# Filler products between the gated levels, a retention output in five parts, and another order on VectorE and GpSimd

## The chip, the cores and the metric

The kernel runs on one core of one Trainium2 chip. The metric is the device time of one execution in microseconds (us). A core has five engines with instruction queues of their own: TensorE (PE in the profile; PEld is its weight load), VectorE (DVE), ScalarE (ACT), GpSimd (POOL) and SyncE (SP), which here only issues transfers. Each runs its instructions in program order, and they wait for one another through semaphores. TensorE's clock has two levels in the profile, 2.4 GHz (granted clock 1.00) and 1.2 GHz (0.50).

## The reference

The reference is two blocks of two layers on 512 tokens of width 1024, all in float32. The change lies in the layers of the first block, and there between the attention and the output projection. Such a layer computes

```python
proj = h @ w_in                                   # aq ak av ag | rq rk rv rg | gq gk gv gg ga
a_out = sliding_window_attention(aq, ak, av, sinks) * silu(ag)
r = retention(rq, rk, rv)                         # 4 heads, chunks of 128 tokens
r_out = rms_norm(r) * silu(rg)
log_a = log_sigmoid(ga @ gla_gate_w + gla_gate_b) / 16
g = gated_linear_attention(gq, gk, gv, log_a)     # 4 heads of 32, chunks of 64 tokens
g_out = rms_norm(g, gla_norm_gain) * silu(gg)
y = concatenate([a_out, r_out, g_out]) @ w_out
x = x + gate * rms_norm(y, post_gain)
```

Retention scans over chunks: `intra` is the masked product of the chunk's queries and keys times its values, `inter` is the decayed queries times a 64x64 state per head that is carried from chunk to chunk. Gated linear attention does the same with a decay of its own for every token and channel: `sc[i, j] = sum_d q[i, d] exp(b[i, d] - b[j, d]) k[j, d]` with b the running sum of log_a. The second block (two layers, each with attention and a feed-forward part) is not touched.

## The kernel before, in words

The program is a list of phases written by hand, and each phase writes the instructions of each engine in a fixed order; there is no scheduler. In a layer of the first block the phases are: norm and transposes, the projection `w_in`, transposes of heads, the attention, the class `Memories` (retention and gated attention), the projection `w_out` and the residual. `Memories` is the subject. It runs once in each of two layers (246 to 295 us and 556 to 606 us of the profile).

The gated scores are computed in six levels, `LEVELS = (32, 16, 8, 4, 2, 1)`, from the far pairs of tokens to neighbours. For level l GpSimd forms distances (`distance`, L2939 and L2940), ScalarE their exponentials (`factor`, L2891), VectorE scales the queries (`scale_queries`, L2787) and GpSimd the keys (L2960). TensorE multiplies them (`level_scores`, L2613: 16 products of 32 rows by 64 columns), and the result is put into the score tile: the first two levels by ScalarE (`copy_level`, L2768), the other four by VectorE (`place`, L2779). The scores of a level go into the same PSUM banks 0 to 3 as those of the level before, so a level waits until that one has been placed. Diagonal scores come first (`own_scores` L2601, `place_own` L2757).

Between the levels TensorE does other work: after level 0 it transposes the decayed keys (L2706, which wait for `g_kd`, L2854, on VectorE), after level 1 come the state updates (`gated_updates`, L2624), after level 2 the whole retention output (`retention_out`: L2586 with the carried states, then L2593 with the chunk's own scores, 16 products that show as 32 records), after level 4 the transposes of the attention output (`mix_turn`, L2653). After level 5 `gated_out` (L2637, L2641) waits for the last `place`. A float32 product is two records in the profile.

Around it: `retained` (L2565) and `keep_retained` (L2726) are the chunk scores of retention, R0 and R1; `retained_updates` (L2575) and `retained_states` (L2731, L2734) its states; `gated_states` (L2744, L2746) those of the gated part; `retained_gates` (L2797) and `retained_means` (L2802) work on the retention output. The groups of `GROUP_NAMES` are results in the PSUM banks 2 and 4 to 7; `open` waits until the group that last used the bank has been taken out of it (kept). `keep_clock(pe, n)` (L254) issues n products of 128 rows by 256 columns whose result nobody reads, by default into bank 7. `weights_low` (L321) splits a weight unit on GpSimd.

## Time and profile before

| | |
|---|---|
| Time, median of three runs | 2465.29 us (2464.46 to 2468.06) |
| The profiled execution | 2465.29 us, span 2463.4 us |
| Busy | PE 2294.8 us (93%), PEld 1972.0 (80%), DVE 1426.3 (58%), ACT 962.4 (39%), POOL 944.0 (38%) |
| Mean granted clock of TensorE | 0.964 |
| First layer's `Memories` | log transposes at 245.21 us, level 0 at 254.87, `gated_out` at 287.19, output projection at 295.18 |
| Second layer's `Memories` | level 0 at 565.36 us, `gated_out` at 597.75 |

A row of the timeline has the start in the span and the duration in us, the engine, the line of the kernel, the operation, what it writes and reads, and in brackets the idle time ahead of it with what ended it. The two layers run the stage alike, 310.5 us apart.

### The profile page before, as it was taken

The page shows a single profiled execution, that of the slowest core. Times are in us where ns is not written, and L with a number is a line of the kernel's source. Part 1 is how long each engine was busy: PE and PEld are TensorE (multiplying, and loading weights), DVE is VectorE, ACT ScalarE, POOL GpSimd, SP SyncE. Part 2 cuts the span into 40 slices and gives each one's busy share as a digit, 9 for nine tenths or more (in the row PEclk, how much of TensorE's full clock was granted, in tenths as well). Part 3 has the DMA queues.
Part 4 walks back from the last instruction along what each step waited for, and adds up shares of the span by engine and source line. Part 5 has one row for each costly group of instructions (what it writes and reads, how often), then busy time and mean ns, then how long its engine had stood idle before and what let it go on. Part 6 is the DMA issues. An engine that isn't in the chain of part 4 may idle for free.

```text
span 2463.4 us, 36101 instructions
## 1 busy us (share of the span) xinstructions
PE 2294.8 (93%) x14294; PEld 1972.0 (80%) x14294; DVE 1426.3 (58%) x2032; ACT 962.4 (39%) x1818; POOL 944.0 (38%) x740
## 2 busy tenths in 40 slices
PE   4998899988899889899999999999899999899998
PEld 4787777877778556679989989898787767789987
DVE  6865536655777654475515234134677765757756
ACT  2335242352234756624221212113425873534433
POOL 3443464434353423416433424334652433321022
PEclk9999699996899999999999999999999999999999
DMA  9650035201433000031423323233441004233332
GB/s 310 192 164 18 19 107 185 86 18 44 145 105 116 2 1 1 10 120 32 135 74 95 103 76 96 86 94 98 147 137 34 1 1 137 78 110 105 95 103 77
DMA packets 163999, 219.11 MB, mean 89 GB/s; under 512 B 19381, under 2 KB 102741, under 8 KB 163705
## 3 DMA queue, kind: packets, MB, share of 16 engines
q1 hardware_dynamic: 163832, 216.82, 28.0%
q8 instruction: 114, 1.87, 0.3%
q14 instruction: 53, 0.43, 0.1%
HBM read 214.69 MB, written 2.10 MB: 88 GB/s over the span
## 4 chain that ended last, share of the span: by engine, by line
PE 56%; DVE 5%; ACT 3%; POOL 2%; issue 2%; DMA 0%; ACTq 0%; DVEq 0%; POOLq 0%; SPq 0%
PE ps L336 14%; PE ps L338 13%; PE ps L337 13%; PE ps L1198 5%; PE ps L1226 4%; PE ps L1248 2%; PE ps L1506 1%; DVE mod_acc_aux L435 1%; PE ps L1245 1%; POOL h_transposed L653 1%; PE ps L461 1%; PE ps L665 0%; ACT att_probs_two L1291 0%; ACT att_probs_lat L1291 0%; PE ps L1501 0%
## 5 line engine op out<-in xcount | busy, mean ns | idle before, releaser
L321 POOL TENSOR_TENSOR w_lo<-w_raw,w_hi 128x1024 fp32r<-128x1024 f32 (+3 forms) x205 | 479.9, 2342 | 1040.1 <-ACT w_hi L315 1040.0
L315 ACT ACTIVATE w_hi<-w_raw 128x1024 fp32r<-128x1024 f32 (+3 forms) x232 | 234.2, 1012 | 836.8 <-PE ps L338 762.6
L336 PE MATMUL ps<-w_hi,h_transposed 128*128 128x512 f32 (+3 forms) x1136 | 422.0, 372 | 25.7 <-POOL w_lo L321 11.7
L337 PE MATMUL ps<-w_lo,h_transposed 128*128 128x512 f32 (+3 forms) x1136 | 413.7, 364 | 0.0
L338 PE MATMUL ps<-w_hi,h_transposed 128*128 128x512 f32 (+3 forms) x1136 | 413.4, 364 | 0.0
L336 PE MATMUL ps<-h_transposed,w_hi 128*128 128x384 f32 (+2 forms) x1048 | 337.0, 322 | 8.0 <-POOL h_transposed L653 3.3
L338 PE MATMUL ps<-h_transposed,w_lo 128*128 128x384 f32 (+2 forms) x1048 | 335.9, 321 | 0.0
L337 PE MATMUL ps<-h_transposed,w_hi 128*128 128x384 f32 (+2 forms) x1048 | 335.9, 320 | 0.0
L336 PEld LDWEIGHTS ps<-w_hi,h_transposed 128*128 128x128 f32 x1136 | 219.3, 193 | 64.4 <-POOL w_lo L321 15.6
L337 PEld LDWEIGHTS ps<-w_lo,h_transposed 128*128 128x128 f32 x1136 | 219.4, 193 | 32.2 <-issue 2.2
L338 PEld LDWEIGHTS ps<-w_hi,h_transposed 128*128 128x128 f32 x1136 | 218.9, 193 | 32.0
L336 PEld LDWEIGHTS ps<-h_transposed,w_hi 128*128 128x128 f32 x1048 | 197.9, 189 | 11.4 <-issue 3.8
L337 PEld LDWEIGHTS ps<-h_transposed,w_hi 128*128 128x128 f32 x1048 | 197.9, 189 | 1.4
L338 PEld LDWEIGHTS ps<-h_transposed,w_lo 128*128 128x128 f32 x1048 | 197.9, 189 | 1.3
L1330 DVE TENSOR_REDUCE attention_stats<-ps 128x1 f32<-128x768 f32 (+5 forms) x192 | 143.8, 773 | 51.5 <-PE ps L1198 43.9
L435 DVE SCALAR_TENSOR_TENSOR mod_acc_aux<-mod_units_one,c_act,mod_acc_aux 128x512 f32<-128x512 f32 x128 | 133.2, 1058 | 42.3 <-DMA mod_units_one<-in_w_mod_dram 31.5
L336 PE MATMUL ps<-w_hi,ffn_hidden 128*128 128x512 f32 x384 | 154.8, 403 | 0.6 <-DVE ffn_hidden L1948 0.6
L338 PE MATMUL ps<-w_hi,ffn_hidden 128*128 128x512 f32 x384 | 153.6, 400 | 0.0
L337 PE MATMUL ps<-w_lo,ffn_hidden 128*128 128x512 f32 x384 | 153.5, 400 | 0.0
L1705 DVE TENSOR_TENSOR ffn_full<-ps,ffn_silu 128x768 f32<-128x768 f32 x22 | 20.0, 953 | 184.2 <-PE ps L338 184.2
L435 DVE SCALAR_TENSOR_TENSOR mod_acc_gates<-w_raw,c_act,mod_acc_gates 128x512 f32<-128x512 f32 x98 | 114.9, 1207 | 12.8 <-DMA w_raw<-in_ada_w_dram 11.2
L336 PEld LDWEIGHTS ps<-w_hi,ffn_hidden 128*128 128x128 f32 x384 | 73.4, 191 | 18.5 <-POOL w_lo_third L321 1.0
(399 smaller groups left out, 4240.2 us busy)
## 6 DMA issues: line engine op xcount, KB each, us to landing
w_raw<-in_ffn_w_in_dram SPq DMA_DIRECT2D x88, 512.0 KB, 3.6
w_raw<-in_ada_w_dram SPq DMA_DIRECT2D x48, 512.0 KB, 4.0
w_raw<-in_ffn_w_out_dram SPq DMA_DIRECT2D x44, 512.0 KB, 3.8
mod_units_one<-in_w_mod_dram SPq DMA_DIRECT2D x80, 256.0 KB, 4.3
w_raw<-in_w_in_dram SPq DMA_DIRECT2D x40, 512.0 KB, 3.8
w_raw<-in_w_out_dram SPq DMA_DIRECT2D x16, 512.0 KB, 4.5
mod_units_one<-in_ada_w_dram SPq DMA_DIRECT2D x32, 256.0 KB, 4.1
mod_unit_even<-in_ada_w_dram SPq DMA_DIRECT2D x16, 512.0 KB, 3.8
```

The costliest lines, as they stand in the source:

```text
L315: act.activation(split_room(i)[0][:, 0:k * n], src[:, 0:k * n], ACT.Copy).then_inc(w_hi_ready.sem, 1)
L321: eng.tensor_tensor(low, src[:, 0:k * n], high.bitcast(F32), ALU.subtract).then_inc(w_lo_ready.sem, 1)
L336: pe.matmul(acc, left[0], right[0], start=start, stop=False, skip_group_check=shared)
L337: pe.matmul(acc, left[0], right[1], start=False, stop=False, skip_group_check=shared)
L338: return pe.matmul(acc, left[1], right[0], start=False, stop=stop, skip_group_check=shared)
L435: ins = dve.scalar_tensor_tensor(out=like(self.acc[:, r]), in0=view[:, j], scalar=c_act[:, cond, 2 * q + j, c:c + 1], in1=like(first if q ...
L461: ins = pe.matmul(ps[:, 6 + m % 2, 4 * i + j:4 * i + j + 1], self.acc[:, i, j * P:(j + 1) * P], ones[:, 0:1], start=True, stop=True)
L653: pool.tensor_tensor(HT[:, 1, kt, tiles[0] * P:tiles[0] * P + n], self.whole(g, kt, tiles), hi.bitcast(F32), ALU.subtract).then_inc(ht_low ...
L1198: done.append(pe.matmul(sc[:, c:c + m], x["q"][i], x["keys"][i][k][0], start=True, stop=not masks))
L1226: ins = pe.transpose(ps[:, self.turn_bank(r), i * P:(i + 1) * P], self.probs[s % len(self.probs)][:, c:c + P], ident)
L1248: ins = pe.matmul(ps[64 * i:64 * i + 64, self.SUM_BANK, 0:P], v[i], probs_t[:, (i * nb + b) * P:(i * nb + b + 1) * P], start=(b == 0), sto ...
L1330: ins = dve.tensor_reduce(dst, src, AX, ALU.max, negate=True)
```

## The change

- **Fillers.** `keep_clock` is called nine times: 3 products before level 0, 1 before and 2 after the transposes of the keys, 2 after the gated updates, 2 after level 2, 1 before level 4, 2 before and 1 after level 5. That is 14 products in each layer.
- **Retention output in five parts.** `retention_carried` after level 2, then four parts of `retention_out(par, two)`: one after level 2, two after level 3, one after level 4. The transposes of the attention output move from before level 5 to behind it.
- **Banks.** The groups have a table of banks (`BANKS`), and `AFTER` names for each the group that must have been taken out first. RU (the retention updates) moves to bank 7 and ahead of SUMS on TensorE. The second bank of the retention output now is the one that held the gated updates, so it opens after `gated_states`; before it opened after the kept keys.
- **VectorE.** `retained_states`, `place_own` and `scale_queries(0)` come before `g_far` (L2849); `keep_retained(R1)` and `scale_queries(1)` before `g_kd`; `place(2)` before `gated_states`; `place(4)` before `retained_gates`.
- **GpSimd.** The second of two `weights_low` moves from the start of the stage behind the gains of level 3. **ScalarE:** `factor(1)` moves before the exponential of `g_far`.

```diff
+            BANKS = [2, 4, 5, 6, 7, 4, 5, 6, 4, 5, 6, 4, 5, 0, 1, 2, 3]
+            AFTER = {SUMS: LOG, R1: R0, R1 + 1: R0 + 1, KD: SUMS, GU: R1, GU + 1: R1 + 1, RO: KD, RO + 1: GU}
+            MIX_BANKS = [6, 4, 5, 7, 0, 1, 2, 3]
+            MIX_AFTER = [GU + 1, RO, RO + 1, RU, OUT, OUT + 1, OUT + 2, OUT + 3]
...
             def open(self, pe, g):
-                if g >= 5:
-                    self.wait_kept(pe, g - 4)
+                if g in self.AFTER:
+                    self.wait_kept(pe, self.AFTER[g])
                 return self.bank(g)
...
-            def retention_out(self, pe):
+            def retention_carried(self, pe):
                 banks = [self.open(pe, self.RO + par) for par in range(2)]
                 self.wait_kept(pe, self.RU)
...
-                self.wait_kept(pe, self.R1 + 1)
-                for par in range(2):
-                    for t in range(XT):
-                        for pair in range(2):
-                            c, v0 = pair * 256 + t * 64, RV + 64 * (2 * pair + par)
-                            ins = pe.matmul(banks[par][:, c:c + 64], ret_a[:, t, par, tok(pair)], P1[:, t, v0:v0 + 64], start=False,
-                                            stop=(t == XT - 1 and pair == 1), skip_group_check=True)
+            def retention_out(self, pe, par, two):
+                self.wait_kept(pe, (self.R1 if two else self.R0) + 1)
+                for t in (2 * two, 2 * two + 1):
+                    for pair in range(2):
+                        c, v0 = pair * 256 + t * 64, RV + 64 * (2 * pair + par)
+                        ins = pe.matmul(self.bank(self.RO + par)[:, c:c + 64], ret_a[:, t, par, tok(pair)], P1[:, t, v0:v0 + 64], start=False,
+                                        stop=(two == 1 and t == XT - 1 and pair == 1), skip_group_check=True)
+                if two:
                     ins.then_inc(mem_made.sem, 1)
...
                 self.retained(pe, self.R1, 1)
+                self.wait_kept(pe, self.RU)
+                keep_clock(pe, 3)
                 self.wait(pe, mem_cleared, 1)
                 for l in range(len(LEVELS)):
                     self.level_scores(pe, l)
                     if l == 0:
                         kd_tok = self.open(pe, self.KD)
+                        keep_clock(pe, 1)
                         self.wait(pe, k_out_ready, 1)
...
+                        keep_clock(pe, 2)
                     if l == 1:
                         self.gated_updates(pe)
+                        keep_clock(pe, 2)
                     if l == 2:
-                        self.retention_out(pe)
+                        keep_clock(pe, 2)
+                        self.retention_carried(pe)
+                        self.retention_out(pe, 0, 0)
+                    if l == 3:
+                        self.retention_out(pe, 1, 0)
+                        self.retention_out(pe, 0, 1)
+                        keep_clock(pe, 1)
                     if l == 4:
+                        self.retention_out(pe, 1, 1)
+                        keep_clock(pe, 2)
+                    if l == 5:
+                        keep_clock(pe, 1)
                         for kt in range(4):
...
                 self.scale_queries(dve, 3)
+                self.place(dve, 2)
                 self.gated_states(dve)
-                self.place(dve, 2)
```

TensorE, first layer, from level 2 (the first rows) to level 3, before. L2586 is the carried part of the retention output, L2593 the chunks' own part.

```order
L2613 MATMUL ps<-proj_one,gla_k_level 128x64 [waits gla_placed] x3
L2613 MATMUL ps<-proj_one,gla_k_level 128x64 x12
L2586 MATMUL ps<-ret_states,ret_qdecay_t 128x64 [waits memory_kept_dve,memory_kept_act]
L2586 MATMUL ps<-ret_states,ret_qdecay_t 128x64 x11
L2593 MATMUL ps<-proj_one,ret_scores_t 128x64 [waits memory_kept_dve]
L2593 MATMUL ps<-proj_one,ret_scores_t 128x64 x15
L2613 MATMUL ps<-proj_one,gla_k_level 128x64 [waits gla_placed,gla_k_level,gla_q_level]
```

And now (L2616 are the level's products, L2587 and L2595 the two kinds of retention output, L254 the fillers):

```order
L2616 MATMUL ps<-proj_one,gla_k_level 128x64 [waits gla_placed] x3
L2616 MATMUL ps<-proj_one,gla_k_level 128x64 x12
L254 MATMUL ps<-static_constants 128x256 x2
L2587 MATMUL ps<-ret_states,ret_qdecay_t 128x64 [waits memory_kept_dve,memory_kept_act]
L2587 MATMUL ps<-ret_states,ret_qdecay_t 128x64 x11
L2595 MATMUL ps<-proj_one,ret_scores_t 128x64 [waits memory_kept_dve]
L2595 MATMUL ps<-proj_one,ret_scores_t 128x64 x3
L2616 MATMUL ps<-proj_one,gla_k_level 128x64 [waits gla_placed,gla_k_level,gla_q_level]
```

Two fillers stand between level 2 and the carried part, and only a quarter of the own part is left ahead of level 3.

VectorE, first layer, from the placing of the diagonal scores to `g_kd`, before (L2849 is `g_far`, L2757 `place_own`, L2854 `g_kd`, L2731 and L2734 the retention states, L2726 `keep_retained`):

```order
L2849 TENSOR_TENSOR gla_distance_to_end<-gla_log_decay_sums 128x512 [waits memory_kept_act]
L2757 TENSOR_TENSOR proj_one<-ps,constants_one 128x512 [waits gla_scored] x4
L2787 TENSOR_TENSOR proj_one<-gla_q_t,gla_factor 128x256 [waits gla_factor]
L2854 TENSOR_TENSOR gla_distance_to_end<-gla_k_t,gla_decay_out 128x512 [waits gla_decays_ready]
L2731 COPY ret_states<-ps 128x128 [waits memory_made]
```

And now, behind the retention states (L2770 is `place_own`, L2865 `g_far`, L2739 `keep_retained`, L2870 `g_kd`):

```order
L2770 TENSOR_TENSOR proj_one<-ps,constants_one 128x512 [waits gla_scored] x4
L2800 TENSOR_TENSOR proj_one<-gla_q_t,gla_factor 128x256 [waits gla_factor]
L2865 TENSOR_TENSOR gla_distance_to_end<-gla_log_decay_sums 128x512 [waits memory_kept_act]
L2739 TENSOR_TENSOR ret_scores_t<-ps,constants_one 128x2x256 [waits memory_made] x2
L2800 TENSOR_TENSOR proj_one<-gla_q_t,gla_factor 128x256 [waits gla_factor]
L2870 TENSOR_TENSOR gla_distance_to_end<-gla_k_t,gla_decay_out 128x512 [waits gla_decays_ready]
```

The scaling for level 0 no longer has `g_far` ahead of it, and `g_kd` has two keeps and the scaling for level 1 ahead of it.

VectorE, first layer, from the scaling of the queries of levels 2 and 3 to the placing of level 2, before (L2744 and L2746 are `gated_states`, L2779 is `place(2)`):

```order
L2787 TENSOR_TENSOR proj_one<-gla_q_t,gla_factor 128x256 [waits gla_scored,gla_factor] x2
L2744 COPY gla_states<-ps 128x64 [waits gla_decays_ready,memory_made]
L2746 SCALAR_TENSOR_TENSOR gla_states<-gla_states,gla_chunk_decay,ps 128x64 [waits dve_step] x6
L2779 COPY_PREDICATED proj_one<-constants_one,ps 128x32x8 [waits gla_placed,gla_scored] x4
L2787 TENSOR_TENSOR proj_one<-gla_q_t,gla_factor 128x256 [waits gla_scored,gla_factor]
```

And now (L2800, L2792, L2757 and L2759 in the same roles):

```order
L2800 TENSOR_TENSOR proj_one<-gla_q_t,gla_factor 128x256 [waits gla_scored,gla_factor] x2
L2792 COPY_PREDICATED proj_one<-constants_one,ps 128x32x8 [waits gla_placed,gla_scored] x4
L2757 COPY gla_states<-ps 128x64 [waits gla_decays_ready,memory_made]
L2759 SCALAR_TENSOR_TENSOR gla_states<-gla_states,gla_chunk_decay,ps 128x64 [waits dve_step] x6
L2800 TENSOR_TENSOR proj_one<-gla_q_t,gla_factor 128x256 [waits gla_scored,gla_factor]
```

The states, for which the carried part on TensorE now waits, stand behind the placing of level 2, and that waits for level 2.

## Rows read from the trace of the kernel before

**Rows 1.** The page: TensorE's granted clock in 40 slices, in tenths
```profile
PEclk9999699996899999999999999999999999999999
```

**Rows 2.** Stretches of both layers: start:end, busy us per engine, PEclk, DMA share, GB/s
```profile
243.00:256.00 13.00, 8.18 (x142) 7.08 (x140) 8.67 (x12) 5.69 (x10) 9.65 (x9) 1.00 0.01 1
257.00:267.00 10.00, 7.70 (x144) 7.25 (x144) 7.23 (x19) 4.88 (x10) 9.53 (x13) 0.50 0.01 2
267.00:276.00 9.00, 9.00 (x68) 8.76 (x66) 0.20 (x1) 1.19 (x2) 0.00 (x0) 0.50 0.01 2
...
284.00:287.00 3.00, 0.58 (x24) 0.45 (x16) 2.39 (x5) 0.00 (x0) 2.02 (x1) 1.00 0.53 199
288.00:297.00 9.00, 9.00 (x59) 8.53 (x49) 3.72 (x9) 1.53 (x4) 0.00 (x0) 0.50 0.01 2
...
568.00:594.00 26.00, 23.60 (x264) 22.32 (x264) 13.56 (x32) 7.57 (x15) 10.28 (x15) 0.50 0.26 78
```

**Rows 3.** Timeline, first layer: start us, us, instruction; in brackets the idle time before
```profile
254.87 1.12 PE L2613 MATMUL ps<-proj_one,gla_k_level 32*128 32x64 f32 x32 [2.98 <-DVE proj_one L2787]
...
258.70 1.98 PE L2613 MATMUL ps<-proj_one,gla_k_level 32*128 32x64 f32 x32 [1.97 <-DVE proj_one L2787]
...
262.55 1.99 PE L2613 MATMUL ps<-proj_one,gla_k_level 32*128 32x64 f32 x32 [0.60 <-ACT proj_one L2768]
...
264.46 2.83 PE L2586 MATMUL ps<-ret_states,ret_qdecay_t 64*128 64x64 f32 x24
...
267.21 7.09 PE L2593 MATMUL ps<-proj_one,ret_scores_t 128*128 128x64 f32 x32
...
276.81 2.87 PE L2613 MATMUL ps<-proj_one,gla_k_level 32*128 32x64 f32 x32 [0.59 <-DVE proj_one L2779]
...
279.61 3.67 PE L2653 MATMUL ps<-static_constants,proj_one 128*128 128x128 f32 x16
```

**Rows 4.** Timeline, first layer: the two kinds of product of gated_out
```profile
287.19 1.21 PE L2637 MATMUL ps<-gla_states,gla_gate_ln 32*64 32x64 f32 x56 [2.61 <-DVE proj_one L2779]
...
288.33 7.09 PE L2641 MATMUL ps<-proj_one 128*128 128x64 f32 x32
```

**Rows 5.** Timeline, first layer: VectorE around the levels
```profile
249.51 2.06 DVE L2849 TENSOR_TENSOR gla_distance_to_end<-gla_log_decay_sums 128x512 f32<-128x512 f32 x1 [1.19 <-ACT gla_log_decay_sums L2885]
...
251.49 2.47 DVE L2757 TENSOR_TENSOR proj_one<-ps,constants_one 128x512 f32<-128x512 f32 x4
...
253.88 0.88 DVE L2787 TENSOR_TENSOR proj_one<-gla_q_t,gla_factor 128x256 f32<-128x256 f32 x1
...
254.69 1.21 DVE L2854 TENSOR_TENSOR gla_distance_to_end<-gla_k_t,gla_decay_out 128x512 f32<-128x512 f32 x1
...
256.13 0.98 DVE L2734 SCALAR_TENSOR_TENSOR ret_states<-ret_states,constants_one,ps 128x64 f32<-128x64 f32 x4
...
257.03 1.28 DVE L2726 TENSOR_TENSOR ret_scores_t<-ps,constants_one 128x512 f32<-128x512 f32 x2
...
263.68 1.86 DVE L2746 SCALAR_TENSOR_TENSOR gla_states<-gla_states,gla_chunk_decay,ps 128x64 f32<-128x64 f32 x6
...
265.46 1.42 DVE L2779 COPY_PREDICATED proj_one<-constants_one,ps 128x256 f32<-128x256 uint32 x4
...
279.30 2.46 DVE L2779 COPY_PREDICATED proj_one<-constants_one,ps 128x256 f32<-128x256 uint32 x4
...
284.61 2.43 DVE L2779 COPY_PREDICATED proj_one<-constants_one,ps 128x256 f32<-128x256 uint32 x4 [1.60 <-PE ps L2613]
```

**Rows 6.** Timeline, TensorE: fillers (L254) and 64-column products at either clock
```profile
241.61 1.69 PE L254 MATMUL ps<-static_constants 128*128 128x256 f32 x4
...
243.13 1.00 PE L1239 MATMUL ps<-proj_one,att_probs_t_one 128*128 128x64 f32 x8
...
341.71 3.61 PE L254 MATMUL ps<-static_constants 128*128 128x256 f32 x16
```

**Rows 7.** Timeline, second layer: TensorE's wait after the output projection's first half
```profile
642.61 3.57 PE L461 MATMUL ps<-static_constants,mod_acc_aux 128*128 128x1 f32 x16 [6.46 <-ACT y_square_junk L1032]
```

More of the change, by code:

```diff
@@ L2528, in __init__ @@
                 self.bank_signal = ht_low
-                self.bank_done = {4 + kt: self.g0 + kt + 1 for kt in range(4)}
-                self.bank_done.update({kt: self.g0 + 5 + kt for kt in range(4)})
+                self.bank_done = {self.MIX_BANKS[kt]: self.g0 + kt + 1 for kt in range(KT)}
                 self.prelude_sp, self.prelude_dve = prelude_one(1) if l == 0 else prelude_even()
@@ L2690, in tensor @@
                 self.retained(pe, self.R0, 0)
+                self.retained_updates(pe)
                 sums = self.open(pe, self.SUMS)
@@ L2846, in vector @@
                 self.keep_retained(dve, self.R0, 0)
+                self.retained_states(dve)
+                self.place_own(dve)
+                self.scale_queries(dve, 0)
                 self.wait_kept(dve, self.SUMS)
@@ L2866, in vector @@
                 self.scale_queries(dve, 5)
+                self.place(dve, 4)
                 self.retained_gates(dve)
-                self.place(dve, 4)
                 self.retained_means(dve)
@@ L2943, in gpsimd @@
                 n = len(LEVELS)
-                for _ in range(2):
-                    weights_low(pool, 2, HALF)
+                weights_low(pool, 2, HALF)
                 self.wait(pool, mem_cleared, 1)
@@ L2965, in gpsimd @@
                             ins.then_inc(gains_ready.sem, 1)
+                            weights_low(pool, 2, HALF)
                 for i, c in enumerate((slice(0, 16), slice(16, 24), slice(24, 32))):
```

27 lines of the change are left out of this document (8 added, 19 removed).

## The prediction

> **What bounds the kernel now.** I read the page's clock row first, then stretches cut where the clock changes, then the timeline of the stage that is changed, first TensorE, then VectorE. The clock row shows a 6 at the fifth and the tenth slice and an 8 behind the tenth: those are the two layers' retention and gated stages [rows 1]. Cut finer, TensorE has 1.00 up to 256 us, 0.50 from 257 on through the levels and the retention output, 1.00 again for the short stretch 284 to 287, and 0.50 for the whole of `gated_out`; the second layer shows the same in 568 to 594 [rows 2]. In 267 to 276 TensorE is busy 9.00 of 9.00 us, nearly all of it the own part of the retention output, while VectorE works 0.20 us and GpSimd nothing [rows 2, 3]. So this stage has two faces: up to level 2 TensorE waits for the others (2.98 us ahead of level 0, 1.97 ahead of level 1, 0.60 ahead of level 2) [rows 3], from there to level 4 it is TensorE at half clock that everybody waits for, and at the end VectorE sets the pace: from the start of place(4) at 279.30 to the end of place(5) at 287.04, 7.74 us with 1.60 idle in it [rows 5], then `gated_out` at 287.19 [rows 4].
>
> A gain here reaches the end. Behind the stage TensorE is the engine that does not stop; the only wait of size is in the second layer, 6.46 us [rows 7], and it hangs on a chain of VectorE that begins after the stage's last transposes, so it moves with the stage.
>
> **Prices at the two clocks.** Four filler records, that is two products, took 1.69 us at half clock (0.85 a product); sixteen took 3.61 at full (0.45 a product). Eight records of 64 columns took 1.00 us at full [rows 6]; 32 of the same form took 7.09 at half, 1.77 for eight [rows 3]. A level's 32 records took 1.12 at full and 1.98 at half [rows 3]. The full clock is thus worth a factor of 1.8.
>
> **The change, step by step, first layer.**
>
> *Before level 0.* RU ahead of SUMS and its states on VectorE cost nothing: they lie in VectorE's 1.19 us of idle ahead of `g_far` [rows 5] (states 0.28 + 0.98); without that cover they would cost 1.3 us. place_own can start about 249.9 instead of 251.49 and takes 2.47, the scaling for level 0 took 0.88, so level 0 starts at about 253.3 instead of 254.87 [rows 3, 5]. The three fillers (3 x 0.45 = 1.4 us at full) lie in TensorE's idle time there. The second weights_low now runs where GpSimd has time; its unit is used two units of the projection later, no cost.
>
> *`g_kd` comes later.* After 253.3 VectorE has `g_far`, the R1 keep 1.28, a scaling about 0.4, `g_kd` 1.21. `g_far` took 2.06 beside the GpSimd split that is now gone; the same shape, `g_kd`, took 1.21 beside GpSimd's short operations [rows 5], and this is the nearer case: 1.2, bounds 0.7 (what two operations of the R1 keep take each, 0.64) and 2.1. Sum: 253.3 + 1.2 + 1.3 + 0.4 + 1.2 = 257.4. The key transposes wait for it, with level 1 queued behind them. With the one filler ahead, TensorE stands idle for most of the 3 us before 257.4, as it does now before 254.87 and 258.70; I expect the clock to fall at the same place, around 256.5. The transposes (about 0.9 at half) and two fillers (1.7) then put level 1 at 260.0, against 258.70.
>
> *The clock comes back early.* Transposes and fillers are the wide products beside which it returned before (242 us: fillers; 283 us: transposes of 128 columns) [rows 3, 6], and 2.6 us of them are one behind the other. At full clock the way from the start of level 1 to that of level 2 shrinks from 3.85 us (262.55 - 258.70) by 0.9 to 3.0, so level 2 begins near 263 and ends near 264.
>
> *A new wait.* The carried part writes to the bank of the gated updates and so waits for gated_states, which VectorE now does after place(2), which waits for level 2: 1.42 + 0.21 + 1.86 = 3.5 us after level 2 [rows 5], minus 0.9 for the two fillers: 2.6 us idle. The carried part begins at 267.4 instead of 264.46 [rows 3]; queued behind it are all products to the end. I expect the clock to fall a second time around here.
>
> *To the end of level 4.* From the carried part to place(4) it was 279.30 - 264.46 = 14.84. Off: one quarter of the own part 1.77, the wait 0.59 ahead of level 4 and the 0.9 by which level 4 (2.87 against 1.99) was slowed by the placing. On: a filler 0.85. That is 12.4, so place(4) starts at 279.8.
>
> *The tail.* place(4) to the end of place(5): the retention gates move into the 1.60 us idle, so 7.4 to 7.7, and `gated_out` starts at 287.4, 0.2 later than now. TensorE has in that time a quarter 1.77, two fillers 1.7, level 5, a filler and the sixteen transposes 3.67: this ends in time only if the clock is back by about 283.6, right after the two fillers. The transposes now stand directly ahead of `gated_out` instead of level 5 and an idle 2.61 us, so the clock is still full in it: 1.2 + 7.09 x 1.00 / 1.81 = 5.1 instead of 8.2, 3.1 less. The projection's first 1.9 us at half clock go, 0.9 less [rows 2, 4].
>
> *Sum.* +0.2 - 3.1 - 0.9 = -3.8 us a layer. In the second layer the same if the clock changes at the same steps. It need not: the same steps at half clock lose most of it (if it comes back only during the transposes, these end at 290, and 2.7 of the 3.8 go). I count two thirds there, 2.5. Together -6.3, and 2465.3 (the profiled execution: span 2463.4 and 1.9 around it, equal to the median) gives 2459.0. All edits with unknown size are in the range: `g_far` at 2.1 puts +0.9 on each layer, at 0.7 takes 0.5 off.
>
> **Rivals.**
>
> B. *The clock holds, or returns early and stays.* Level 1 at 258.8, level 2 at 261.8, carried part at 266.5; 12.4 at full clock is about 6.7, place(4) at 273.2, `gated_out` at 280.7: -6.5 and the 4.0 of the tail, 10.5 a layer: 2444.3. For it: fourteen fillers. Against it: the two idle stretches before 257.4 and before 267.4 stay, and 3.0 us of idle time is what preceded the fall at 256. The Trainium skill ("TensorE: Matmul & The Clock Gate", Part 1) says that the gate follows how busy TensorE has been and that activity releases it; by that alone this rival would be the likely one, since from the carried part on TensorE hardly stops. The trace disagrees: 9.00 busy of 9.00 us went by at 0.50 with the 64-column products [rows 2].
>
> C. *Slower: the fillers are paid at half clock.* If the clock does not come back after the key transposes, level 1 is at 260.0, level 2 at 263.9, the carried part at 269.4, place(4) at 281.8 and its end 289.3. TensorE after level 4 has 1.77 + 1.7 + 1.99 + 0.85 + 3.67 = 10.0 and reaches `gated_out` at 292.1, 4.9 later. If `gated_out` then runs at half too, both layers cost 9.8: 2475. If it runs at full, 0.9 a layer: 2467. It decides from the point where the clock is still 0.50 when `gated_out` begins. For it: the fillers are 8.5 us at half clock in the part that was never idle. Against it: the transposes brought the clock back before.
>
> D. *One gain, one loss.* The clock is back in one layer in time, in the other during the transposes or later: -3.8 and -1.1 to +4: 2460 to 2466, no change that can be told.
>
> **How the numbers follow.** What can be told from no change is 0.2%, 4.9 us. Forecast 0.40 (own range 2454 to 2463), B 0.12, C 0.18 (0.06 of it at the 2467 end), D 0.30. Faster: 0.40 x 0.9 + 0.12 + 0.30 x 0.2 = 0.54. Slower: 0.12 of C and 0.03 for mishaps of D: 0.15. Same: 0.31. The range runs from near B's end to just over C's cheap end, 2446 to 2469, and leaves out about half of B and 0.1 of C.
>
> **What would show it.** Right: level 0 near 253.3, key transposes near 257.4, an idle time of about 2.6 us ahead of the carried part ended by the state update on VectorE, place(4) near 279.8, `gated_out` near 287.4 and 5 us long at clock 1.00. Wrong: the clock at 1.00 through levels 3 and 4 (B), or 0.50 in `gated_out` (C); no idle time ahead of the carried part would void the step of the new wait.

## The result, and the profile after

The changed kernel took 2469.77 us (median of 20 runs, 2463.80 to 2474.43), the kernel before in the same job 2464.38 us (20 runs, 2460.53 to 2468.08): ratio 1.0020, 95% interval 1.0013 to 1.0028. The forecast was 2459.0, faster. It went the other way by 0.20%, and the time lies just above the range. All times and ratios here are of executions in the chip's faster state; one of e13's twelve, 3050.75 us at a granted clock of 0.70, is left out of its ratio. The profiled execution has a span of 2469.2 us against 2463.4.

The page's clock row after (tenths of full speed, 40 slices) still has its low places at the fifth, tenth and eleventh slice, as in [rows 1]:

```profile
PEclk9999799997899999999999999999999999999999
```

Stretches of the changed kernel, in the columns of [rows 2]:

```profile
239.00:249.00 10.00, 8.93 (x55) 7.85 (x56) 2.33 (x5) 6.27 (x8) 4.09 (x4) 0.50 0.00 0
249.00:259.00 10.00, 6.99 (x112) 5.62 (x108) 9.20 (x18) 4.92 (x9) 7.67 (x11) 1.00 0.01 2
260.00:262.00 2.00, 2.00 (x9) 1.17 (x12) 0.90 (x2) 0.60 (x1) 2.00 (x3) 0.50 0.00 0
263.00:269.00 6.00, 4.31 (x108) 3.21 (x102) 3.05 (x10) 2.65 (x6) 3.59 (x4) 1.00 0.01 3
270.00:293.00 23.00, 23.00 (x176) 20.34 (x176) 10.78 (x22) 3.62 (x6) 5.64 (x5) 0.50 0.17 49
294.00:297.00 3.00, 3.00 (x28) 3.00 (x28) 0.85 (x2) 0.93 (x3) 0.00 (x0) 1.00 0.00 0
584.00:607.00 23.00, 22.98 (x176) 20.58 (x176) 10.79 (x22) 3.51 (x6) 5.87 (x5) 0.50 0.24 71
```

In this execution the clock came back early, as forecast (1.00 in 263 to 269), but not for long. From 270, where the carried part is at work, it is 0.50 for 23 us, in which TensorE is busy 23.00 of 23.00 us; the second layer shows the same. It is full again in `gated_out`, which was at 0.50 before.

TensorE's timeline in the first layer, answering to [rows 3, 4] (L2616 are the levels, L2711 the key transposes, L254 the fillers, L2587 the carried and L2595 the own part, L2657 the mix transposes, L2640 and L2644 `gated_out`, L336 the output projection):

```profile
252.68 1.56 PE L254 MATMUL ps<-static_constants 128*128 128x256 f32 x6
254.78 1.12 PE L2616 MATMUL ps<-proj_one,gla_k_level 32*128 32x64 f32 x32 [0.54 <-DVE proj_one L2800]
255.83 0.70 PE L254 MATMUL ps<-static_constants 128*128 128x256 f32 x2
259.07 1.08 PE L2711 MATMUL ps<-static_constants,gla_distance_to_end 128*128 128x128 f32 x4 [2.54 <-DVE gla_distance_to_end L2870]
259.94 1.92 PE L254 MATMUL ps<-static_constants 128*128 128x256 f32 x4
261.79 1.47 PE L2616 MATMUL ps<-proj_one,gla_k_level 32*128 32x64 f32 x32
...
265.12 1.12 PE L2616 MATMUL ps<-proj_one,gla_k_level 32*128 32x64 f32 x32
266.17 1.13 PE L254 MATMUL ps<-static_constants 128*128 128x256 f32 x4
269.78 2.83 PE L2587 MATMUL ps<-ret_states,ret_qdecay_t 64*128 64x64 f32 x24 [2.48 <-issue]
...
279.82 1.17 PE L254 MATMUL ps<-static_constants 128*128 128x256 f32 x2
...
284.60 2.02 PE L254 MATMUL ps<-static_constants 128*128 128x256 f32 x4
...
288.46 1.22 PE L254 MATMUL ps<-static_constants 128*128 128x256 f32 x2
289.48 3.62 PE L2657 MATMUL ps<-static_constants,proj_one 128*128 128x128 f32 x16
293.03 0.95 PE L2640 MATMUL ps<-gla_states,gla_gate_ln 32*64 32x64 f32 x56
293.91 3.79 PE L2644 MATMUL ps<-proj_one 128*128 128x64 f32 x32
297.50 0.48 PE L336 MATMUL ps<-w_hi,h_transposed 128*128 128x512 f32 x1
...
300.81 0.50 PE L336 MATMUL ps<-w_hi,h_transposed 128*128 128x512 f32 x1 [1.67 <-DVE h_transposed L2666]
```

Two idle stretches of 2.5 us stand ahead of the key transposes and of the carried part, and behind the first six products of the projection is a stall that the kernel before does not have. VectorE's timeline at the same places, answering to [rows 5]:

```profile
257.81 1.21 DVE L2870 TENSOR_TENSOR gla_distance_to_end<-gla_k_t,gla_decay_out 128x512 f32<-128x512 f32 x1
...
266.23 1.42 DVE L2792 COPY_PREDICATED proj_one<-constants_one,ps 128x256 f32<-128x256 uint32 x4
267.56 0.22 DVE L2757 COPY gla_states<-ps 128x64 f32<-128x64 f32 x1
267.82 1.86 DVE L2759 SCALAR_TENSOR_TENSOR gla_states<-gla_states,gla_chunk_decay,ps 128x64 f32<-128x64 f32 x6
...
282.92 2.44 DVE L2792 COPY_PREDICATED proj_one<-constants_one,ps 128x256 f32<-128x256 uint32 x4 [4.73 <-PE ps L2616]
...
299.28 0.68 DVE L2837 TENSOR_REDUCE head_squares<-proj_one 128x8 f32<-128x512 f32 x1
299.99 0.17 DVE L2804 TENSOR_SCALAR head_meansq<-head_squares 128x8 f32<-128x8 f32 x1
300.07 1.28 DVE L2666 TENSOR_TENSOR h_transposed<-ps,h_transposed 128x512 fp32r<-128x512 f32 x2
```

The states end at 267.82 + 1.86 = 269.68, 0.10 before the carried part starts, and the carried part's bank opens when they are done: I take that for the wait of 2.48, for which the row names no engine ("issue"). In e3 and e6, where the states come earlier, it is gone. The stall at 300.81 ends with the first of the two `mix_low` at 300.07: the projection's second tile writes bank 5, which in the new numbering held mix transpose 2, and VectorE reads that out behind both `gated_means`.

In the profiled execution the difference can be placed. From the log transposes to the output projection it was 50.0 us in both layers before; it is 52.3 (245.25 to 297.50) and 51.7 after: +4.0. Behind it each layer pays the stall of 1.67 and saves 0.75 by a projection that no longer starts at half clock: +1.8. The spans differ by 5.8. Between the layers the changed kernel loses 1.0 us more and behind the second it gains 1.0 back, which I have not traced.

Within the layer, before and after (first layer): log transposes to level 0, 9.7 and 9.5 us; level 0 to the carried part, 9.6 and 15.0; the carried part to `gated_out`, 22.7 and 23.3; `gated_out` to the projection, 8.0 and 4.5. So the stage loses 5.4 us by the two waits and the fillers up to the carried part, gains 3.5 by `gated_out` at full clock, and in between, where the change should have gained, it loses 0.5.

### The profile page after: what moved, and what is told of

Read it like the earlier page. It is cut to its first block, busy times and chain, and to the rows that moved or that the text cites. A ratio compares the mean times of both kernels' runs of the same rounds, so it can differ in the third digit from the quotient of the medians.

```text
span 2469.2 us, 36213 instructions
## 1 busy us (share of the span) xinstructions
PE 2304.2 (93%) x14350; PEld 1974.2 (80%) x14350; DVE 1427.0 (58%) x2032; ACT 962.4 (39%) x1818; POOL 946.4 (38%) x740
## 4 chain that ended last, share of the span: by engine, by line
PE 55%; DVE 5%; ACT 3%; issue 2%; POOL 2%; DMA 1%; ACTq 0%; DVEq 0%; POOLq 0%; SPq 0%
PE ps L336 13%; PE ps L338 13%; PE ps L337 13%; PE ps L1198 5%; PE ps L1226 4%; PE ps L1248 2%; DVE mod_acc_aux L435 1%; PE ps L1506 1%; PE ps L1245 1%; POOL h_transposed L653 1%; PE ps L665 0%; ACT att_probs_two L1291 0%; ACT att_probs_lat L1291 0%; PE ps L461 0%; PE ps L1501 0%
## 5 line engine op out<-in xcount | busy, mean ns | idle before, releaser
L336 PE MATMUL ps<-w_hi,h_transposed 128*128 128x512 f32 (+3 forms) x1136 | 422.1, 372 | 30.9 <-POOL w_lo L321 11.9
L336 PE MATMUL ps<-h_transposed,w_hi 128*128 128x384 f32 (+2 forms) x1048 | 338.2, 323 | 8.8 <-POOL h_transposed L653 3.4
L336 PEld LDWEIGHTS ps<-w_hi,h_transposed 128*128 128x128 f32 x1136 | 219.3, 193 | 70.7 <-issue 16.4
L336 PEld LDWEIGHTS ps<-h_transposed,w_hi 128*128 128x128 f32 x1048 | 198.6, 190 | 12.1 <-issue 3.8
L336 PE MATMUL ps<-w_hi,ffn_hidden 128*128 128x512 f32 x384 | 153.3, 399 | 0.6 <-DVE ffn_hidden L1948 0.6
L336 PEld LDWEIGHTS ps<-w_hi,ffn_hidden 128*128 128x128 f32 x384 | 72.5, 189 | 18.1 <-POOL w_lo_third L321 1.0
```

Source lines behind the costliest of these rows:

```text
L336: pe.matmul(acc, left[0], right[0], start=start, stop=False, skip_group_check=shared)
```

## The experiments

Each was timed in five rounds beside the kernel before, 4 to 12 executions each. The medians come from several jobs, in which the kernel before took 2462.5 to 2465.0 us, so kernels are compared by their ratios; 0.001 is 2.5 us. The last column is the time from the log transposes to the output projection in each layer of the one execution that was profiled.

```
kernel                                    median    ratio [95%]               layer 1 / 2, us
before                                    2464.4    1                         50.0 / 50.0
changed                                   2469.8    1.0020 [1.0013, 1.0028]   52.3 / 51.7
e1  changed, no fillers                   2456.9    0.9979 [0.9968, 0.9990]   47.5 / 46.8
e4  before + 13 fillers a layer           2456.0    0.9979 [0.9964, 0.9994]   42.8 / 54.7
e2  changed, mix_low early                2468.0    1.0025 [1.0012, 1.0038]   52.1 / 52.2
e3  changed, states ahead of place(2)     2459.8    0.9999 [0.9987, 1.0011]   40.7 / 50.7
e6  changed, states and mix_low early     2456.1    0.9977 [0.9958, 0.9997]   40.5 / 43.8
e7  changed, no fillers behind level 2    2465.6    1.0003 [0.9991, 1.0016]   50.3 / 49.0
e12 changed, first stretch filled         2462.1    0.9991 [0.9981, 1.0001]   47.6 / 47.6
e13 changed, second stretch filled        2458.5    0.9980 [0.9967, 0.9992]   45.6 / 45.7
e8  changed, both stretches filled        2443.6    0.9925 [0.9906, 0.9945]   40.3 / 40.3
e14 fillers in idle stretches alone       2452.2    0.9959 [0.9943, 0.9975]   41.0 / 42.2
e5  no fillers, states and mix_low early  2449.9    0.9947 [0.9929, 0.9965]   43.4 / 43.4
e9  e8, mix_low early                     2443.4    0.9912 [0.9898, 0.9925]   41.9 / 40.2
e10 e12, states and mix_low early         2443.0    0.9912 [0.9898, 0.9926]   40.0 / 39.8
e11 before + 22 fillers a layer           2443.7    0.9908 [0.9894, 0.9923]   38.9 / 38.9
```

### The two halves of the change, each alone

**e1**: all calls of `keep_clock` in the levels removed, the new order kept. They are eight, with 14 products; that they are nine, as the section on the change and some expectations have it, is a miscount.

> The changed kernel without its nine calls of keep_clock (14 products a layer), all else kept. Theory 1 (the fillers are paid at half clock from level 3 on, where TensorE has no idle time): three groups of them, 1.17 + 2.02 + 1.22 us in the first layer behind level 3, lie on TensorE's way to gated_out, so about 2 us a layer less than the changed kernel: near 2465.5. Theory 2 (the fillers bring the clock back after the key transposes and save more than they cost): level 1 to the end of level 2 runs at half clock, the carried part begins later or at the same time, and the kernel is slower than the changed one: 2472 to 2475. The wait ahead of the carried part grows to about 3.3 us under both.

Measured: 0.9979. Both theories missed. The new order alone gains 5 us, so the fillers cost the changed kernel 0.0041, 10 us; the clock is at 0.50 from 252.6 to 286.7 and comes back behind the mix transposes, as `gated_out` begins (285.9), all the same. That is where the order's gain lies: `gated_out` takes 4.6 and 4.4 us in the two layers, 8.0 before, and the layers as a whole are 2.5 and 3.2 us shorter.

**e4**: the kernel before with fillers, nothing else.

```diff
                 self.retained(pe, self.R1, 1)
+                self.wait_kept(pe, self.SUMS)
+                keep_clock(pe, 3)
...
                         kd_tok = self.open(pe, self.KD)
+                        keep_clock(pe, 1)
...
+                        self.wait_kept(pe, self.RU)
+                        keep_clock(pe, 2, 4)
```

The last two lines stand behind the key transposes; 2 more products follow behind each of levels 1 and 2, 1 behind level 3 and 2 behind level 4.

> The kernel before with fillers alone: 3 products before level 0, 1 before and 2 after the key transposes, 2 after the gated updates, 2 after level 2, 1 after level 3, 2 before the transposes of the attention output (13 a layer; into banks that are free there), no other edit. If the fillers do bring the clock back after the key transposes and nothing makes TensorE idle ahead of the carried part, the clock stays at 1.00 through the retention output: some 6 us a layer less than before, near 2453. If they are paid at half clock like the ones behind level 3 of the changed kernel, the kernel is 3 to 6 us a layer slower than before: 2470 to 2476.

Measured: 0.9979, 5 us less, half of the gain that was expected if the clock came back. Its layers went apart: 42.8 us with the clock at 1.00 from 259 to 272, over the whole retention output, and 54.7 with it at 0.50 from 559 to 589, where the fillers only cost. Either half alone gains 5 us, both together lose 5. So something in the new order turns the fillers from a gain into a price; e3 and the runs that fill one stretch or both look for it.

### The stall behind the projection's start

**e2**:

```diff
                 self.mix_low(dve, 1)
+                self.mix_low(dve, 2)
+                self.mix_low(dve, 3)
...
                 self.gated_means(dve, 1)
-                self.mix_low(dve, 2)
-                self.mix_low(dve, 3)
```

> The changed kernel with mix_low(2) and mix_low(3) on VectorE directly behind mix_low(1), ahead of retained_norm and gated_gates instead of behind the gated means. Theory 1 (the wait of 1.67 and 1.66 us that TensorE has after the first tile of the output projection, for VectorE's h_transposed, is on the way to the end, because the new table of banks makes the second tile wait for the third transposed group): 3.3 us less than the changed kernel, near 2466.5, and no such wait in the trace. Rival (it is made up by a later wait, the second half of the projection or the turn of the gated heads): the same as the changed kernel, 2469.8.

In the trace the stall is gone, and the projection's start to the second group of mix transposes takes 5.6 us (296.86 to 302.44) in place of 7.5 (297.50 to 305.04). Timed, the ratio cannot be told from the changed kernel's. e9, where the clock holds and runs scatter less, has the same edit on top of e8:

> The kernel with both idle stretches filled (nine more filler products than the changed kernel), and mix_low of banks 2 and 3 directly behind that of bank 1. That kernel measured 2443.6. Theory 1 (the second group of mix transposes waits for its bank, 7.5 us from the output projection's start in place of 5.5, and this reaches the end): 2443.6 - 2 x 1.7 = 2440, first projection product to second group of transposes 5.5 to 5.9 us. Rival (the work of the projection was in hand anyway, TensorE waits later by the same): 2443 to 2444, with a wait of 1.5 us elsewhere ahead of the next units.

2443.4 against 2443.6, intervals that overlap: the rival's time. What the stall costs at the end is between nothing and some 3 us for both layers by the intervals of e2 and the changed kernel; more these runs do not settle.

### The wait ahead of the carried part

**e3**:

```diff
-                self.place(dve, 2)
                 self.gated_states(dve)
+                self.place(dve, 2)
```

> The changed kernel with gated_states ahead of place(2) on VectorE again, as before the change, all else kept. Theory 1 (the idle 2.48 us ahead of the carried part is what the new bank costs, and it is also where the clock falls for good): the states run straight behind the scaling of level 3's queries, the carried part begins about 1.6 us earlier and the idle time shrinks to about 0.9 us; with the clock falling anyway 1.6 us a layer less, near 2466.5; if the shorter idle time leaves the clock at 1.00 through the retention output, up to 5 us a layer less, near 2460. Rival (level 3, which now waits for place(2) behind the states, takes back what the carried part gains): same as the changed kernel, 2469.8.

Measured: 0.9999, by the ratio 5 us less than the changed kernel, between theory 1's two cases. Its stretches 267 to 287 and 568 to 592 show two answers in one execution:

```profile
267.00:287.00 20.00, 17.36 (x246) 15.26 (x246) 14.56 (x31) 5.43 (x11) 6.13 (x6) 1.00 0.19 56
568.00:592.00 24.00, 24.00 (x180) 20.66 (x179) 11.82 (x25) 3.17 (x6) 6.94 (x6) 0.52 0.22 67
```

The first layer keeps 1.00 from level 2 on and takes 40.7 us; in the second it is 0.50 from level 1 to `gated_out`, and the layer takes 50.7. 10 us a layer hang on the clock, the 10.5 of rival B.

**e6** goes further: the states ahead of the scaling of level 3, and `mix_low` as in e2.

> The same two moves on VectorE, with all fillers of the changed kernel kept. Theory 1 (fillers are paid at half clock wherever TensorE is not idle): it is slower than the kernel without fillers by the fillers that lie behind level 2, some 4 us a layer: 2451 + 8 = 2459, with the clock at 0.50 in most of the levels. Rival (without the idle time ahead of the carried part the fillers hold the clock at 1.00 behind level 2, as in the first layer of the run with the states first): level 2 to gated_out takes 17 us instead of 27 in both layers, 2445 to 2450.

Measured 2456.1, between the two forecasts: its runs lie between 2446 and 2466, with a mean granted clock between 0.965 and 0.977. The wait ahead of the carried part is gone, but 2.54 us ahead of the key transposes are left, and the clock holds in some executions and not in others.

### Filling one stretch, the other, both

**e12**, **e13** and **e8** are the changed kernel with more fillers; e12 has the first edit, e13 the second, e8 both.

```diff
                         kd_tok = self.open(pe, self.KD)
-                        keep_clock(pe, 1)
+                        keep_clock(pe, 5)
...
                     if l == 2:
-                        keep_clock(pe, 2)
+                        keep_clock(pe, 7)
```

> The changed kernel with four more fillers ahead of the key transposes alone; the idle stretch of 2.5 us ahead of the carried part stays. Theory 1 (each idle stretch drops the clock by itself, and the second is the one that costs, since the tail behind it stays at half clock): 1.00 through levels 0 to 2, 0.50 from the carried part to gated_out in at least one layer, 2460 to 2466. Rival (the first fall is the one that matters, the clock that is full ahead of the second stretch outlives it): 1.00 to gated_out in both layers, 2444 to 2448.

Theory 1: 2462.1. The timeline of e12, and its stretches 257 to 267 and 267 to 287:

```profile
267.13 2.50 PE L2587 MATMUL ps<-ret_states,ret_qdecay_t 64*128 64x64 f32 x24 [2.48 <-issue]
...
281.61 2.02 PE L254 MATMUL ps<-static_constants 128*128 128x256 f32 x4
```
```profile
257.00:267.00 10.00, 6.84 (x138) 5.14 (x136) 6.50 (x16) 3.44 (x8) 9.22 (x11) 1.00 0.01 2
267.00:287.00 20.00, 19.87 (x163) 17.54 (x164) 8.46 (x19) 1.82 (x3) 5.09 (x6) 0.51 0.20 57
```

The first fall is gone, the second comes behind the 2.48 us of idle time, and TensorE, busy 19.87 of 20.00 us, does not get the clock back.

> The changed kernel with five more filler products ahead of the carried part alone; the idle stretch of 2.5 us ahead of the key transposes stays. Theory 1 (the fall at the second stretch costs the most, 24 us at half clock behind it; the one at the first stretch is mended by the key transposes and fillers in 3.4 us and costs some 2 us a layer): 1.00 from level 2 to gated_out, 2443.6 + 4 = 2447 to 2448. Rival (both must be filled, since the clock that has just come back falls again sooner): 2455 to 2462, 0.50 from the carried part on in one layer or both.

2458.5: the rival's time, but with 1.00 from the carried part on, as theory 1 had it. The clock falls at the first stretch and stays low for 13 us (258.4 to 271.4), where in the profile of the changed kernel it was back after 3. The added fillers come later and cannot be the reason. The changed kernel, e2, e3, e6, e7 and e13 run the same on TensorE up to level 2, and in their twelve profiled stages the clock was back ahead of level 2 in seven: in all six whose log transposes ran at 0.50, and in one of the six where they ran at 1.00. Where it was not back, level 0 to the carried part took 17.1 us (first layers of e2 and e7) instead of 15.0, since the fillers there ran at half clock too; without any it took 14.7 (e1). The seven fillers ahead of the carried part, 14 records, take 4.63 us instead of 3.29 as in e8, and from there the clock is full to `gated_out`:

```profile
269.03 4.63 PE L254 MATMUL ps<-static_constants 128*128 128x256 f32 x14
273.59 1.55 PE L2587 MATMUL ps<-ret_states,ret_qdecay_t 64*128 64x64 f32 x24
```

> The changed kernel with four more filler products ahead of the key transposes and five more ahead of the carried part, so that neither idle stretch is left. Theory 1 (the clock falls behind idle time, and comes back late: without idle time it holds): 1.00 from level 0 to gated_out in both layers, levels 2 to 5 and the output at full clock, 8 to 10 us a layer less, some 2452. Rival (the clock falls at these products whatever fills the gaps): the fillers take 0.85 us each at half clock, nine of them 7.7 us, of which about 5 lie in the gaps: 2.7 a layer more, 2475.

Theory 1, and by more: 0.9925, some 19 us less than before. The timeline of e8, and the stretches 257 to 267, 267 to 287 and 568 to 592:

```profile
251.15 1.12 PE L2616 MATMUL ps<-proj_one,gla_k_level 32*128 32x64 f32 x32 [0.55 <-DVE proj_one L2800]
252.20 2.42 PE L254 MATMUL ps<-static_constants 128*128 128x256 f32 x10
255.44 0.66 PE L2711 MATMUL ps<-static_constants,gla_distance_to_end 128*128 128x128 f32 x4 [0.81 <-DVE gla_distance_to_end L2870]
...
260.92 3.29 PE L254 MATMUL ps<-static_constants 128*128 128x256 f32 x14
264.53 1.56 PE L2587 MATMUL ps<-ret_states,ret_qdecay_t 64*128 64x64 f32 x24 [0.32 <-issue]
```
```profile
257.00:267.00 10.00, 9.68 (x170) 8.27 (x170) 4.27 (x14) 3.28 (x7) 8.83 (x10) 1.00 0.01 2
267.00:287.00 20.00, 16.70 (x241) 14.62 (x240) 15.43 (x32) 4.80 (x10) 5.37 (x3) 1.00 0.20 57
568.00:592.00 24.00, 20.70 (x260) 17.99 (x261) 17.05 (x34) 5.15 (x11) 7.54 (x5) 1.00 0.34 112
```

The waits for VectorE are the same as in the changed kernel; TensorE only computes while it waits. That it is the idle time and not the number of wide products that counts, e10 (below) supports: there the second stretch is not filled but taken away, and the clock holds up to `gated_out` as well. Filled alone, the first stretch is worth 7 us and the second 10; together they are worth 23, since a clock lost at one is no longer there to keep at the other.

### The fillers between the levels

**e7**: the changed kernel without the fillers behind levels 3, 4 and 5.

> The changed kernel without the four filler products behind levels 3 and 4 and ahead of the mix transposes; the other ten stay. Theory 1 (these are paid at half clock, 1.17 + 2.02 + 1.22 = 4.4 us a layer in the changed kernel's trace, and bring the clock back not earlier than the transposes would): 2469.8 - 8.8 = 2461. Rival (the early fillers are what costs, or the late ones bring back the clock for gated_out, whose products take 7.09 us at half and 3.79 at full clock): 2469 to 2476, gated_out at 0.50 in one layer or both.

Half of theory 1: 1.0003, 4 us less than the changed kernel instead of 8.8. From the carried part to `gated_out` it is 20.2 us in both layers instead of 23.3: 3.1, not 4.4. The fillers' rows overlap their neighbours (from start to start they are 4.1 us), and level 5 now runs beside the placing of level 4 and takes 2.65 us instead of 1.99. At half clock these fillers are paid; the timed difference of 4 us is just at the edge of the noise, the trace's 3.1 us a layer is clearer.

**e14**: the same four products off, and those behind the key transposes and level 1 too; 3 stand ahead of level 0, 5 ahead of the key transposes, 7 ahead of the carried part.

> The changed kernel with fillers in its three idle stretches alone: 3 ahead of level 0, 5 ahead of the key transposes, 7 ahead of the carried part; none behind the key transposes, level 1, level 3, level 4 and level 5. Theory 1 (the idle stretches alone drop the clock; the fillers between the levels, which are what the change adds, aren't needed): 1.00 to gated_out in both layers, 2441 to 2444. Rival (the products of 64 columns do not hold the clock by themselves, whatever stands ahead of them): it falls behind level 1 or in the retention output, 2450 to 2458.

2452.2, the rival's time, though the clock fell later than it said. Two stretches of the first layer, and the timeline of the second:

```profile
267.00:275.00 8.00, 7.80 (x122) 7.43 (x122) 3.35 (x10) 1.34 (x3) 3.12 (x5) 1.00 0.03 4
275.00:287.00 12.00, 11.86 (x139) 10.93 (x139) 9.69 (x19) 4.38 (x9) 2.94 (x1) 0.72 0.32 94
```
```profile
578.39 1.96 PE L2657 MATMUL ps<-static_constants,proj_one 128*128 128x128 f32 x16
582.30 0.89 PE L2640 MATMUL ps<-gla_states,gla_gate_ln 32*64 32x64 f32 x56 [1.95 <-DVE proj_one L2787]
583.12 7.09 PE L2644 MATMUL ps<-proj_one 128*128 128x64 f32 x32
```

In the second layer the clock holds up to the mix transposes and falls in `gated_out`, which has 7.09 instead of 3.79. In the first it falls at 275.9, in the middle of level 5, with TensorE busy 7.80 of the 8 us before and no idle stretch since the one of 0.32 ahead of the carried part; it is back for `gated_out`. So idle time is not the only thing that precedes a fall: products of 64 columns without fillers between them did not keep the clock up here either. The fillers between the levels keep 8 us once the clock is up (e8 against e14), and the late ones cost some 4 us where it is down (the changed kernel against e7).

### Versions that beat both kernels

**e5**: e1 with the two moves of e6.

> The changed kernel without its nine filler calls, with the gated states ahead of the scaling of level 3 on VectorE, and with mix_low of banks 2 and 3 directly behind that of bank 1. Theory 1 (the fillers, the wait ahead of the carried part and the wait of the second group of mix transposes are three costs that add up): the kernel without fillers measured 2456.9; without the wait of 2.5 us a layer the levels start 1 to 2 us earlier, without that of the transposes 1.6 us a layer goes: 2456.9 - 2 x (1.5 + 1.6) = 2451, no idle time over 0.5 us ahead of the carried part. Rival (VectorE sets the pace: what the states gain the placings lose, since the same instructions stand in another order): only the 1.6 a layer or nothing is gained, 2453.5 to 2457.

2449.9, theory 1: without one filler 13 us less than before, at half clock through all levels (253 to 283). This is what the new order is worth if its own wait is taken out. Of the 6.6 us that each layer is shorter, 3.6 are again `gated_out` at full clock (4.4 us instead of 8.0), behind mix transposes that now stand directly ahead of it; the other 3.0 are the order itself.

**e10**:

> The changed kernel with four more fillers ahead of the key transposes, none added ahead of the carried part, the gated states ahead of the scaling of level 3 on VectorE, and mix_low of banks 2 and 3 directly behind that of bank 1. Theory 1 (the wait ahead of the carried part is a price beside the clock: with the states early the fillers there are not needed, and the carried part starts about 2 us earlier at the same clock): clock 1.00 from level 0 to gated_out in both layers, 38.5 us from the log transposes to the projection in place of 40.3, 2440 - 2 x 1.8 = 2436. Rival (VectorE is the bound at full clock: the placings only wait for each other): 40 us, 2440. A second rival (the clock falls in one layer): 2445 to 2450.

2443.0, which can't be told from e8 and fits the first rival's 2440 no better than theory 1's 2436: the carried part does come 2.5 us earlier after the log transposes (18.8 us against 21.3), but the layers take 40.0 and 39.8 us. The clock falls in `gated_out` in both layers (279.6 to 289.8 in the first), behind an idle time of 1.49 us ahead of it that e8 has too; in e8 it held, and the runs do not show why. `gated_out` takes 6.7 and 6.4 us in place of 4.4, which is what theory 1 lacks.

**e11**: the kernel before, its order and banks unchanged, with more fillers than e4, and the first four mix transposes behind level 5.

> The kernel before, its order on VectorE and GpSimd and its banks unchanged, with 22 filler products a layer (6 ahead of level 0, 1 ahead of and 2 behind the key transposes, 2 behind level 1, 3 behind level 2, 2 behind level 3, 4 behind level 4, 2 behind level 5), and the first four mix transposes behind level 5 instead of level 4. Theory 1 (what the kernel before lacks is the clock, not the order): 1.00 from level 0 to gated_out, no wait for states ahead of the carried part and none ahead of the second mix transposes, 39 to 41 us from the log transposes to the projection in place of 50.0 in both layers: 2464 - 2 x 9.5 = 2445 or below. Rival (the new order is what lets the clock hold: the own part of 32 products of 64 columns in one piece lets it fall whatever is in the gaps): 0.50 from the own part on, 2452 to 2460.

2443.7, theory 1. Its stretches 257 to 267 and 267 to 287, and the own part in one piece:

```profile
257.00:267.00 10.00, 9.48 (x170) 7.57 (x168) 8.06 (x22) 5.58 (x11) 10.00 (x15) 1.00 0.02 3
267.00:287.00 20.00, 19.85 (x255) 17.72 (x254) 14.43 (x30) 4.80 (x10) 4.17 (x4) 1.00 0.21 57
```
```profile
266.35 3.79 PE L2593 MATMUL ps<-proj_one,ret_scores_t 128*128 128x64 f32 x32
```

The old order takes 38.9 us a layer with the clock held, the new one 40.3 (e8). The new one reaches level 0 after 8.0 us instead of 9.7, but takes 13.4 from there to the carried part instead of 9.4, and then 14.6 to `gated_out` instead of 15.5. So at full clock the moves on VectorE bring nothing in sum, and the retention output needs no cutting. e8, e9, e10 and e11 are equal within their intervals, some 0.8 to 0.9% faster than before.

## Why the prediction was wrong, step by step

*Before level 0: right where the clock was full.* With the clock full at the entry, the log transposes to level 0 take 8.0 us (e8: 243.19 to 251.15) instead of 9.7, the 1.6 forecast. In the profiled execution of the changed kernel TensorE came out of the attention at 0.50, up to 249, and level 0 began at 254.78, not 253.3.

*`g_kd` later: right.* `g_far` took 1.21 as chosen, and the key transposes came 4.29 us after the start of level 0; forecast 4.1. The fall of the clock in that wait was forecast too.

*The clock comes back early: right in both layers of the profile, and worth little.* Level 1 to level 2 took 3.33 us, forecast 3.0. The other profiles show that it does not always come back (seven of twelve stages, see e13).

*A new wait of 2.6 us ahead of the carried part: right*, 2.48 in both layers, and with it the second fall, which I had expected too. What I priced was its 2.6 us of time. Its real price was the clock: 23 us at 0.50 behind it. Filled with work that nobody needs, in e8 against e12, the same wait costs 16 us less.

*The fillers' price at half clock: too low.* The 1.69 us for two products [rows 6], 0.85 each, were read from a stretch in which the clock rose at 242.9. Wholly at half clock two products took 2.02 us (284.60 in the changed kernel), about 1.0 each.

*The tail: this is the step that failed.* I had the clock "back by about 283.6, right after the two fillers". It was at 0.50 until 293.3 in the first layer and until 607.3 in the second, and the fillers were paid there: 1.17 + 2.02 + 1.22 us. `gated_out` began at 293.03, not at 287.4. Of the 5.6 us, 1.5 are the entry, 1.6 came from there to place(4) (282.92, forecast 279.8), 2.5 between it and `gated_out` (10.1 us, forecast 7.6). From the carried part to `gated_out` I had 20.0 us, 2.7 less than before; it took 23.3, more than before. The gain of `gated_out` at full clock did come, 4.5 us instead of 8.0. This comes nearest to the mild end of rival C, which I had at 2467 and a chance of 0.06: "the fillers are paid at half clock", `gated_out` full. But C's condition, that the clock does not come back after the key transposes, did not hold in the profile: it came back and fell again at the new wait, as the forecast itself had it. What failed is the second return. I had taken the return at the mix transposes before the change [rows 3] as what two fillers would do; in the changed kernel two fillers behind level 4 didn't do it in either layer.

*The bank table: not priced at all.* It put a wait of 1.67 us a layer into the projection, which nothing in my steps names. It is part of the difference in the trace, though its share of the measured time isn't settled (e2, e9).

*Rival B* was at 2444.3 with 0.12. The change as written was not it; the change with both waits filled is, at 2443.6. My argument against it, two idle stretches that stay, was right. The Trainium skill ("TensorE: Matmul & The Clock Gate", Part 1, "HAM oscillation") tells of a kernel in which TensorE waits some 3 to 5 us for DMA, is throttled meanwhile, and starts the next work slow. In e12 and e8 a wait of 2.48 us for VectorE was enough, with 0.51 in 267 to 287 behind it and 1.00 where it was filled. The Trainium skill ("TensorE: Matmul & The Clock Gate", Part 1) also says that activity releases the throttle; here the traces do not agree, since e12 was busy 19.87 of those 20.00 us at 0.51, e8 16.70 at 1.00.

## What to carry to other kernels

Before fillers are added, find every wait of TensorE in the stage, the ones that the same change creates too, and fill those first; in this kernel a wait left open in the middle made the fillers behind it a price. Judge a reordering at both clocks: here it was worth 13 us where the levels ran at half clock (7 of them by `gated_out` at full clock) and nothing where the clock held. Renumbering PSUM banks is an edit of the order, and each bank's last reader must be looked up for the stage that comes next.

## What the hardware showed that I had not expected

- Two and a half microseconds of idle time decided over 20 us of clock: 0.51 in 267 to 287 with it (e12), 1.00 without (e8); idle stretches of 0.55 and 0.81 in e8 did no harm, and of 1.49 none in e8 and a fall in e10. In the first layer of e14 the clock fell with no idle stretch in the 8 us before.
- Stretches that were mostly products of 64 columns did not bring the clock back (23.00 busy of 23.00 us at 0.50 in the changed kernel; 9.00 of 9.00 with no other product in it before [rows 2, 3]), but such products ran at 1.00 for 3.79 us in one piece when it was up (e11).
- One kernel can hold the clock in one layer and lose it in the other, in the same execution: 40.7 and 50.7 us (e3), 42.8 and 54.7 (e4). A single profile of such a kernel says little on its mean time.
